# A per-layer gate projection as one fp32 pass, or as three rounded passes with weight blocks parted by GpSimd

## The reference, cut to what matters

```python
    # end of the first block
    gate = jax.nn.sigmoid(rmsnorm(h, g_ple) @ w_pg)      # (512 x 1024) @ (1024 x 1024)
    h = h + (p @ w_pe) * gate
    x = rmsnorm(h, g_final)
    # start of the second block
    mod = silu(c) @ ada_w[0] + ada_b[0]
    sh1, sc1, g1, sh2, sc2, g2 = jnp.split(mod, 6, axis=-1)
    h = rmsnorm(x, norm_mix[0]) * (1 + sc1) + sh1
    y = gla_mixer(h, ...)
```

## Time and profile before

| | us |
|---|---|
| median of three timed runs | 3770.45 |
| span of the profiled execution, which the trace covers | 3769.0 |
| PE busy | 2808.7 (75%) |
| POOL (GpSimd) busy | 2176.5 (58%) |
| DVE (VectorE) busy | 1531.3 (41%) |
| ACT (ScalarE) busy | 678.8 (18%) |

### The profile page before, as it was taken

One profiled execution on the slowest core, in us unless ns is written; L12 is line 12 of the kernel. 1 busy time (PEld: TensorE's weight loads), 2 busy tenths in 40 slices (PEclk: granted clock), 3 DMA queues, 4 the chain that ended last, 5 costly groups with the idle time before them and its releaser, 6 DMA issues.

```text
span 3769.0 us, 33937 instructions
## 1 busy us (share of the span) xinstructions
PE 2808.7 (75%) x9169; PEld 1697.0 (45%) x9169; DVE 1531.3 (41%) x3068; ACT 678.8 (18%) x1345; POOL 2176.5 (58%) x1973
## 2 busy tenths in 40 slices
PE   7449936665666655666556687998999977889998
PEld 5325712222222222222222333766787853468876
DVE  3541175555655555555655345023211033521110
ACT  2022211111111111111111122113211032311101
POOL 4884466665666656665666486903555538145653
PEclk9768968888888888888888887988999988899999
DMA  3132288988998889998999642511232224013221
GB/s 97 53 115 78 68 315 321 330 325 312 325 328 328 316 306 339 327 326 290 331 336 332 222 162 90 178 45 35 78 100 86 92 78 151 12 56 100 94 94 68
DMA packets 294761, 719.89 MB, mean 191 GB/s; under 512 B 24820, under 2 KB 149666, under 8 KB 294706
## 3 DMA queue, kind: packets, MB, share of 16 engines
q0 software_dynamic: 160512, 587.27, 43.4%
q1 hardware_dynamic: 134194, 131.92, 11.0%
HBM read 717.02 MB, written 2.10 MB: 191 GB/s over the span
## 4 chain that ended last, share of the span: by engine, by line
PE 44%; issue 14%; DVE 13%; POOL 9%; DMA 6%; ACT 2%; DVEq 1%; POOLq 1%; ACTq 0%; SPq 0%
PE ps L534 9%; PE ps L537 8%; PE ps L541 8%; POOL arena L1104 8%; DMA arena<-in_expert_u_dram,arena 5%; PE ps L706 4%; PE ps L485 3%; PE ps L584 2%; PE ps L803 2%; PE ps L496 1%; DVE arena L1804 1%; DVE arena L1805 1%; POOL arena L1097 1%; DVE arena L1806 1%; DVE arena L1803 1%
## 5 line engine op out<-in xcount | busy, mean ns | idle before, releaser
L706 PE MATMUL ps<-arena,nT 128*128 128x512 f32 x2048 | 1008.8, 641 | 593.4 <-ACT nT L1341 425.2
L706 PEld LDWEIGHTS ps<-arena,nT 128*128 128x128 f32 x2048 | 398.2, 204 | 1201.6 <-issue 752.4
L1850 DVE CUSTOM_DVE_ANT_0 arena<-arena,ps 128x1024 f32<-128x1024 f32 x512 | 625.1, 1221 | 497.0 <-DMA arena<-in_expert_u_dram,arena 444.7
L1104 POOL DMA_INDIRECT arena<-in_expert_u_dram,arena x512 | 488.5, 954 | 283.7 <-POOL arena L1097 204.5
L1104 POOL DMA_INDIRECT arena<-in_expert_v_dram,arena x512 | 484.3, 946 | 166.3 <-issue 162.3
L1057 POOL TENSOR_SCALAR whi_f<-wring 128x2048 fp32r<-128x2048 f32 (+1 forms) x60 | 125.2, 2087 | 329.4 <-DMA wring<-in_ffn_w_in_dram 204.3
L1061 POOL TENSOR_TENSOR wlo<-wring,whi_f 128x2048 fp32r<-128x2048 f32 (+1 forms) x60 | 302.2, 5037 | 11.0 <-POOL whi_f L1057 11.0
L537 PE MATMUL ps<-n_hi,wlo 128*128 128x512 f32 x1024 | 260.2, 397 | 2.1 <-POOL wlo L1061 2.1
L537 PEld LDWEIGHTS ps<-n_hi,wlo 128*128 128x128 f32 x1024 | 196.7, 192 | 46.2 <-POOL wlo L1061 3.7
L2033 DVE TENSOR_TENSOR arena<-ps,arena 128x512 f32 x44 | 30.4, 692 | 409.1 <-PE ps L541 409.1
L1030 POOL TENSOR_TENSOR arena<-arena 128x1024 f32<-128x1024 f32 x96 | 189.3, 1972 | 7.5
(11 more groups left out here) (299 smaller groups left out, 3687.8 us busy)
## 6 DMA issues: line engine op xcount, KB each, us to landing
arena<-in_ada_w_dram POOLq DMA_DIRECT2D x48, 1024.0 KB, 5.8
wring<-in_ffn_w_in_dram SPq DMA_DIRECT2D x44, 1024.0 KB, 5.1
wring<-in_ffn_w_out_dram SPq DMA_DIRECT2D x16, 1408.0 KB, 6.2
wring<-in_gla_w_in_dram SPq DMA_DIRECT2D x12, 1024.0 KB, 5.4
wring<-in_w_in_dram SPq DMA_DIRECT2D x9, 1024.0 KB, 5.3
wring<-in_w_q_dram SPq DMA_DIRECT2D x8, 1024.0 KB, 5.4
arena<-in_expert_u_dram,arena POOLq DMA_INDIRECT x512, 5.8
arena<-in_expert_v_dram,arena POOLq DMA_INDIRECT x512, 6.0
```

The costliest lines, as they stand in the source:

```text
L706: mm = e.matmul(ps[:, 6 + q, :], diag[:, k, :], ring[:, s, q * 512:(q + 1) * 512], start=False, stop=stop)
L1104: e.indirect_dma_start(ring[:, s, :], None, table, bass.IndirectOffsetOnAxis(ap=cur[:, s:s + 1], axis=0)).then_inc(landed[s].sem, 16)
L1850: e.tensor_tensor_reduce(junk, ring[:, s, :], ps[:, 4:6, :].rearrange("p a k -> p (a k)"), 1.0, 0.0, ALU.mult, ALU.add, dots[:, k:k + 1]). ...
```

## The change

The gate projection is done by `split_linear` in place of `linear`. Four things are added for it. Two high buffers `whi_p` lie behind the other tensors of that stage. GpSimd parts the four units of w_pg, in its list between its wait for `h_ready` 2 and `ada(1)`. ScalarE makes high parts of the normalised activations, and VectorE the low parts.

```diff
@@ buffers of the per-layer embedding
         sgT = R.take(DC, T)
+        whi_p = rounded_pair("whi_p", (R.at, R.at + DC * UNIT), DC * UNIT)
@@ tensor
             squares(DC, 4)
-            linear(4, DC, nrhs, act, norm_chunks(3))
+            split_linear("w_pg", 4, whi_p, n_hi, n_lo, act, operand())
             squares(DC, 4)
             squares(DC, 4)
@@ gpsimd
             e.wait_ge(S["h_ready"], 2)
+            split_run("w_pg", [(4, DC)], whi_p)
             ada(1)
@@ scalar
             root()
+            high_parts(n_hi, norm_chunks(3))
             units(4, copy_to(sgT, func=ACT.Sigmoid))
@@ vector
             rms(hT, nT, lambda k: col("g_ple", k), DC)
+            low_parts(n_hi)
             done.add(8)
```

## The result

The changed kernel takes 3832.94 us (median of four runs, 3830.13 to 3837.11) against 3770.52: a ratio of 1.016, interval 1.0145 to 1.0175. On another chip, beside some of the other kernels of this study, it took 3832.25 against 3768.63, ratio 1.0193, interval 1.016 to 1.0226. The ratios in this document are the recorded ones, which are not the quotient of the two medians: that would be 1.017 here, and one of the four runs took 3851.12. The profiled execution has a span of 3833.4 us and a device time of 3835.02.

The account below looks back on a forecast made before the run. TensorE's chain was taken to bound the kernel, GpSimd's matvec 11.3 us off it. Sums 63.0 us later, -0.5 for their stretch, +0.5 for the rank product: +63 on 3769.0, 3832.0; with 1.45 for the median 3833.5, range 3822 to 3848.

Parts of the forecast that it names:

- The sums: TensorE's modulation sums ahead of the rank product: start 63.0 us later, at 2369.4, and take 7.75 to 8.85 us.
- The slack of 11.3 us: Before the change GpSimd's matvec ends at 2295.14 and TensorE reads it at 2306.42, so it is 11.3 us off the chain.
- The start of the matvec: GpSimd's matvec, behind four partings and their waits, starts at 2241.3 in place of 2162.72, 78.6 us late.
- Its length: GpSimd's moved matvec takes 128 us, between 124.2 and 132.4, and ends at 2369.3.
- The rival of 16.4 us: GpSimd loses each port turn to VectorE's 22 instructions in the moved matvec: 16.4 us, not 4; +12 us, 3846; chance 0.07.
- The idle time: TensorE stands idle for some 50 us ahead of the modulation sums, released by GpSimd's last addition.
- The rank product: TensorE's 16 records behind the sums, 9.04 us before: +0.5 us out of -1.8 to +4.7 after the idle time.
- The gate's 11.6 us: Gate product in three passes, taken alone, ends at 2251.2 in place of 2262.75, 11.6 us earlier.
- The give-back of 5 to 10 us: Second block's own waits, with 60 us to get ready, give back 5 to 10 us: about 3826; chance 0.06.
- The hidden parting: GpSimd's parting is hidden, the matvec ends about 2295, the kernel gains the gate's 11.6 us: 3759; chance 0.02.
- the gate did what it says: Rival at the gate: rounded passes slowed by low clock or late low parts, adding 6 us: 3839.5; chance 0.04.

## Why the prediction was right

**Forecast and result.** 3833.5 was forecast, 3832.94 measured. The direction, the place and the size come from one mechanism, and the experiments hold it: with the wait for the sums moved, 40 us come back; with GpSimd relieved of the parting, 49; with its work alone added, the rank product moves by 17. The sums started 61.2 us later, not 63.0, and took 1.9 us longer than I allowed, so that at the rank product the two errors cancel (+62.7 against +62.5). That the total is met within 0.6 us is luck: behind the rank product differences of 3.5 to 8 us, not forecast, nearly cancel.

**The slack of 11.3 us.** Borne out by the added scratch work: it moved the matvec's start by 28.2 us and the sums by 15.9, with a matvec 1.2 us shorter, which leaves 11.1.

**The start of the matvec.** I had unit 3 parted 78.8 us after the experts' end, and it was ready after 78.1. Within it two errors cancel. The norm ended 2.0 us sooner than I had it (43.0 after the experts' end), since the landings took 5.0 us instead of 5.6 and the w_pe product took 15.39 us instead of 17.27. Why the product was shorter is open: it took 15.62 with the matvec's blocks beside it and 17.26 without, in two other kernels. The first bank took 6.6 us after the norm's end instead of 5.7.

**Its length.** 128 forecast, 127.0 measured. GpSimd did not lose its turns: during the matvec VectorE had 23 instructions with two inputs (22 were allowed for), and GpSimd needed 2.8 us more than in the earlier trace rows. The rival of 16.4 us falls. Its opposite was there: the norm of g_final took 18.17 us and that of norm_mix 18.43, hidden behind the wait. The Trainium skill (SBUF — State Buffer, section "Who interferes with whom") says that the order of issue decides who blocks. The trace agrees where it can be seen, as at the first chunk of g_final's norm, which starts inside GpSimd's product and ends 0.6 us after it, 2.96 us long in place of 0.74:

```profile
2270.09 3.61 POOL L1028 TENSOR_TENSOR arena<-arena,cT 128x2048 f32<-128x2048 f32 x1
2271.30 2.96 DVE L1646 SCALAR_TENSOR_TENSOR hT<-hT,par,row 128x512 f32<-128x512 f32 x1 [13.38 <-ACT row L1200]
```

Why GpSimd so rarely came second here, and VectorE so often, no run settles.

**The idle time.** TensorE stood idle for 70.64 us, where I wrote some 50. I had counted from the end of the norm, forecast around 2320, and the idle time begins at the end of the last squares at 2299.8. The last norm ended at 2332.3, some 10 us later after the experts' end than I had it, still hidden behind the matvec.

**The sums.** Here a term was mis-sized: 10.37 us in both profiles, where I took up to 8.85. The row I took as the worst had a clock above the low level; after 70 us of idle time all 48 ran at it. The rank product took 8.47 us where I allowed 9.5, which makes up 1.1 of the 1.9 us behind that point. At full clock the same 48 take 5.42 us, as one of the kernels with moved sums shows.

**The gate's 11.6 us.** Right as measured here (the product ends 12.4 us sooner, squares 2 start 10.2 sooner), but I read it as the worth of three passes, and it is not. About 5 us are, by the pair without the matvec. The rest lies at the norm, which started 1.9 us sooner and took 8.88 us in place of 13.36, with GpSimd parting unit 1 during its first half and then waiting. That this accounts for the rest is argued from these rows; no run isolates it.

**The rivals.** The give-back of 5 to 10 us did not take place as I had it, by work that was got ready. The attention stage was 4.5 to 8 us shorter, mostly by the clock, and MLA's 3.5 to 6.9 us, by the clock too, took them back. Whether either of these belongs to the change is not settled; differences of this size appear between other kernels of the study. The hidden parting did not occur, and the gate did what it says.

## What to carry to other kernels

Work that is put ahead of something in an engine's list costs its own length plus each wait in it, and a ring of two slots turns the consumer's pace into such waits: 27 us of work moved the matvec by 78. Before adding it, look for the first in-order reader of what stands behind, and for how much slack that reader leaves. Here moving that one reader gave back 40 us, while the addition is worth about 5. An engine off the chain may still be what slows the chain: here it cost VectorE's norms 19.5 us, and stopping it for three short stretches, with the reader moved, gave the only gain of the study among the kernels that compute the whole result, of 0.4%.

## What the runs showed of the hardware

A VectorE norm of eight 128x512 chunks with two inputs took 5.39 us alone and 12.4 to 20.8 us where it lay wholly beside GpSimd's matvec. Eight low parts took 4.90 alone and up to 19.78 beside it, and the eight additions with one tensor input behind the norm (L1656) 3.25 alone and 11.37 beside it. GpSimd's chain of 124 us got 2.8 us longer in the changed kernel and at most 5.8 before. I had expected the loss to be shared.

TensorE ran 48 one-column matmuls in 5.42 us at a granted clock of 1.00, in 7.75 at 0.67 around them, and in 10.37 at 0.50, after 8.80 us of idle time as well as after 70.64.
